# Turning half of x and the cross keys by square transposes and DMAs instead of TensorE

## The chip, the cores and the metric

The kernel runs on one NeuronCore of a Trainium2 chip (trn2). The metric is the device time of one execution, in microseconds, as the median of three runs. The kernel before takes 882.25 us (881.65 to 883.29).

## What is computed

Two transformer layers over 256 tokens of width 1024, in float32. The first mixes a gated delta rule with an indexed sparse attention and ends in a squared-relu feed-forward; the second mixes retention with a forgetting attention, then attends to 256 memory rows, then ends in a gated feed-forward. Cut to the places that the change touches:

```
x  = x + square(relu(rms_norm(x) @ w_mlp_up)) @ w_mlp_down      # first feed-forward
h  = rms_norm(x, g_mix_2);  p = h @ w_in_2                      # x is wanted with features on partitions
q, k, v, gate (retention), q, k, v, f (forgetting) = split(p)
mem: kv = rms_norm(mem, g_mem_2) @ w_xkv_2;  k = rms_norm per head of 256, * g_xk
x  = x + mixed @ w_out_2
q  = rms_norm(rms_norm(x, g_xattn_2) @ w_xq_2 per head of 256) * g_xq
x  = x + (softmax(q @ k.T / 16) @ v) @ w_xo_2                   # 4 heads, 256 memories
x  = x + (silu(h @ w_gate_2) * (h @ w_up_2)) @ w_down_2
```

In the first layer the delta rule needs the inverses of 16 triangular 128x128 matrices (two halves of the tokens, eight heads). The kernel builds them from solved 16x16 bases by products of blocks that double in size.

## The kernel before

It is written by hand: each engine has its own instruction list, and named semaphores order them. The order on an engine is the order of its code; nothing is planned at run time.

**Matrix products.** Every large product runs as three products of two-part numbers: `w_hi` and `w_lo` are the high and low part of the weights, `s_hi` and `s_lo` those of the activations, and hi*hi, hi*lo and lo*hi are summed in PSUM. A product is cut into blocks of up to 512 output columns (`B_DN`, `B_DN + 1`, `B_2`, ...), a block into chunks of 512 rows of the weight matrix, and the chunks go round four slots. SyncE loads a chunk into its slot when the products of the chunk four places earlier are finished (L450); ScalarE writes `w_hi` (L1303); VectorE writes `w_lo` (L1872); TensorE works on a chunk in two quarters of 12 products each (L540). `begin(b)` in ScalarE's and VectorE's lists stands for the splits of the chunks that block b still lacks and of the first two of block b+1; `project` copies a finished block out of PSUM, `residual` adds it to x.

**Turning.** A product wants the activations with features on partitions, and x lies with tokens on partitions. So after each residual TensorE turns x by 16 transposes of 128x128 against the identity into four PSUM banks, four to a bank (`turn`, L603). ScalarE scales them by the norm's gain into `s_hi` (`turn_hi`, L1342) and VectorE writes the rest into `s_lo` (`turn_lo`, L1909). The cross keys and queries are turned by TensorE too (`cross_operands`, L1191), and ScalarE and VectorE copy them out.

**Squares and DMAs.** The memory rows, the retention operands and the hidden rows of the last feed-forward go another way: VectorE transposes each 32x32 square in place (`turn_squares`, L1927) and GpSimd issues 16 DMAs that carry the squares to their bands of 32 partitions (`move`, L373).

**The order around the change.** While block `B_DN + 1` runs (eight chunks), ScalarE and VectorE split its weights. Then x is finished, TensorE turns it and runs `B_2`. ScalarE's list behind the turn: the load of the retention weights (1.5 MB, `act.dma_start(WR, ret_w)`), the squares for two norms, the splits of `B_2 + 1`. GpSimd moves the memory blocks in four bands, one behind each of four splits. VectorE rotates the retention queries and keys (L1937 to L1942) behind `project(B_2 + 1)` and then splits `B_2 + 3`. In the cross attention TensorE runs `B_XQ`, waits for the scaled keys (`x_k`), turns them (16 transposes), runs quarter 0 of `B_XQ + 1`, turns two query operands, runs quarter 1, and then starts `cross_logits(0)` (L1213). In the inverse, TensorE makes the products of step 0 (L921), waits for copies of ScalarE (L1594) and VectorE (L2283), makes those of step 1 (L922), turns the queries p = 2 and 3 (`queries_back`, L796), and runs quarter 2 of `B_GA`.

## Time and profile before

| | |
|---|---|
| median of 3 runs | 882.25 us (881.65 to 883.29) |
| the profiled execution | 883.71 us, its span 881.9 us |
| instructions | 12721 |
| TensorE busy | 873.5 us, 5023 matmuls and transposes |
| VectorE busy | 601.1 us |
| ScalarE busy | 439.4 us |
| GpSimd busy | 183.2 us |
| granted TensorE clock, mean | 0.998 |

The span is the time between the first and the last instruction of the profiled execution; the execution's own time is 1.8 us longer. Busy times are sums of an engine's instructions. Matmuls overlap each other, so their mean length is more than the step from one to the next; for the cost of one, the step is what counts. A row of a timeline merges instructions of one kind and gives start, length and, in square brackets, the idle time before it with what ended it.

### The profile page before, as it was taken

The page shows a single profiled execution, that of the slowest core. Times are in us where ns is not written, and L with a number is a line of the kernel's source. Part 1 is how long each engine was busy: PE and PEld are TensorE (multiplying, and loading weights), DVE is VectorE, ACT ScalarE, POOL GpSimd, SP SyncE. Part 2 cuts the span into 40 slices and gives each one's busy share as a digit, 9 for nine tenths or more (in the row PEclk, how much of TensorE's full clock was granted, in tenths as well). Part 3 has the DMA queues.
Part 4 walks back from the last instruction along what each step waited for, and adds up shares of the span by engine and source line. Part 5 has one row for each costly group of instructions (what it writes and reads, how often), then busy time and mean ns, then how long its engine had stood idle before and what let it go on. Part 6 is the DMA issues. An engine that isn't in the chain of part 4 may idle for free.

```text
span 881.9 us, 12721 instructions
## 1 busy us (share of the span) xinstructions
PE 873.5 (99%) x5023; PEld 751.7 (85%) x5023; DVE 601.1 (68%) x875; ACT 439.4 (50%) x613; POOL 183.2 (21%) x214
## 2 busy tenths in 40 slices
PE   9999999999999999999999999999999999999998
PEld 6897888888988999988888789888888888888886
DVE  5478988998696666745454948977785566665742
ACT  6365456864545555533344426546554544443531
POOL 0432234863110000000004222100100024444500
PEclk9999999999999999999999999999999999999999
DMA  8874542445146655655569765523542567775862
GB/s 297 200 258 144 191 144 87 132 129 166 48 139 195 193 191 190 190 191 191 190 212 258 201 165 192 189 98 118 170 142 79 164 199 218 219 220 160 254 218 72
DMA packets 87651, 154.67 MB, mean 175 GB/s; under 512 B 10528, under 2 KB 18512, under 8 KB 87472
## 3 DMA queue, kind: packets, MB, share of 16 engines
q1 hardware_dynamic: 80352, 144.55, 51.1%
q0 software_dynamic: 4720, 5.86, 3.7%
q10 hardware_dynamic: 2528, 3.56, 1.2%
q8 instruction: 35, 0.57, 0.3%
q14 instruction: 16, 0.13, 0.0%
HBM read 147.53 MB, written 1.44 MB: 169 GB/s over the span
## 4 chain that ended last, share of the span: by engine, by line
PE 92%; DVE 5%; DMA 1%; ACT 1%; issue 1%; SPq 0%; DVEq 0%; ACTq 0%
PE gemm L540 68%; PE gemm L1048 5%; PE mixbank L1048 5%; DVE w_lo L1872 2%; PE mixbank L603 1%; PE mixbank L702 1%; DMA raw<-in_w_in_dram 1%; PE mixbank L727 1%; PE mixbank L808 1%; PE mixbank L1213 1%; DVE mix L2010 1%; PE gemm L1241 1%; PE mixbank L713 1%; PE mixbank L750 1%; PE mixbank L902 0%
## 5 line engine op out<-in xcount | busy, mean ns | idle before, releaser
L1872 DVE TENSOR_TENSOR w_lo<-raw,w_hi 128x2048 fp32r<-128x2048 f32 (+3 forms) x132 | 288.0, 2189 | 180.3 <-ACT w_hi L1303 180.1
L1303 ACT ACTIVATE w_hi<-raw 128x2048 fp32r<-128x2048 f32 (+3 forms) x140 | 255.4, 1833 | 204.7 <-DMA raw<-in_w_in_dram 57.1
L540 PE MATMUL gemm<-w_hi,s_hi 128*128 128x512 f32 (+3 forms) x784 | 208.6, 386 | 0.6 <-ACT s_hi L1339 0.3
L540 PE MATMUL gemm<-w_lo,s_hi 128*128 128x512 f32 (+3 forms) x784 | 201.9, 378 | 1.2 <-DVE w_lo L1872 1.2
L540 PE MATMUL gemm<-w_hi,s_lo 128*128 128x512 f32 (+3 forms) x784 | 202.1, 378 | 0.0
L540 PEld LDWEIGHTS gemm<-w_lo,s_hi 128*128 128x128 f32 x784 | 142.6, 188 | 29.2 <-DVE w_lo L1872 2.1
L540 PEld LDWEIGHTS gemm<-w_hi,s_lo 128*128 128x128 f32 x784 | 143.2, 189 | 27.7
L540 PEld LDWEIGHTS gemm<-w_hi,s_hi 128*128 128x128 f32 x784 | 140.5, 189 | 26.0 <-issue 1.7
L2743 POOL TENSOR_TENSOR sm<-sm 128x2 f32<-128x2 f32 (+5 forms) x13 | 21.6, 1663 | 400.9 <-DVE sm L1933 296.5
L373 POOL DMA_DIRECT2D hid_moved<-hid_blocks x96 | 54.7, 578 | 72.4 <-DVE hid_blocks L2685 70.1
L2737 POOL TENSOR_TENSOR w_lo<-raw,w_hi 128x2048 fp32r<-128x2048 f32 x8 | 36.8, 4614 | 36.1 <-ACT w_hi L1303 36.1
L1320 ACT ACTIVATE mix<-gemm,sm 128x512 f32<-128x512 f32 (+2 forms) x25 | 16.2, 649 | 41.7 <-PE gemm L540 41.7
L1048 PE MATMUL mixbank<-u_lo,w_hi 128*128 128x256 f32 x128 | 35.9, 280 | 0.0
L1048 PE MATMUL mixbank<-s_hi,w_lo 128*128 128x256 f32 x128 | 35.7, 279 | 0.0
L1048 PE MATMUL mixbank<-s_hi,w_hi 128*128 128x256 f32 x128 | 35.6, 278 | 0.0
L540 PE MATMUL gemm<-w_hi,hT_hi 128*128 128x512 f32 x128 | 34.7, 389 | 0.0
L540 PE MATMUL gemm<-w_hi,hT_lo 128*128 128x512 f32 x128 | 34.7, 389 | 0.0
L540 PE MATMUL gemm<-w_lo,hT_hi 128*128 128x512 f32 x128 | 34.7, 389 | 0.0
L1048 PE MATMUL gemm<-u_lo,w_hi 128*128 128x256 f32 x128 | 33.6, 280 | 0.0
L1048 PE MATMUL gemm<-s_hi,w_hi 128*128 128x256 f32 x128 | 33.5, 279 | 0.0
L1048 PE MATMUL gemm<-s_hi,w_lo 128*128 128x256 f32 x128 | 33.5, 279 | 0.0
L2137 DVE SCALAR_TENSOR_TENSOR mix<-mixbank,cw,mix 128x255 f32<-128x255 f32 (+2 forms) x72 | 29.0, 474 | 1.2 <-ACT mix L1465 1.2
(365 smaller groups left out, 1183.8 us busy)
## 6 DMA issues: line engine op xcount, KB each, us to landing
raw<-in_w_in_dram SPq DMA_DIRECT2D x40, 1024.0 KB, 5.2
raw<-in_w_mlp_up_dram SPq DMA_DIRECT2D x16, 1024.0 KB, 5.6
raw<-in_w_mlp_down_dram SPq DMA_DIRECT2D x16, 1024.0 KB, 5.1
raw<-in_w_gate_dram SPq DMA_DIRECT2D x10, 1024.0 KB, 5.3
raw<-in_w_up_dram SPq DMA_DIRECT2D x10, 1024.0 KB, 5.1
raw<-in_w_down_dram SPq DMA_DIRECT2D x10, 1024.0 KB, 5.4
raw<-in_w_out_dram SPq DMA_DIRECT2D x8, 1024.0 KB, 5.2
raw<-in_w_xkv_dram SPq DMA_DIRECT2D x8, 1024.0 KB, 5.1
```

The costliest lines, as they stand in the source:

```text
L373: eng.dma_start(d[32 * j:32 * j + 32, :, i, :], s[32 * i:32 * i + 32, :, j, :]).then_inc(sem(name), 16)
L540: return nc.tensor.matmul(G[b % 2][t][:, 0:width], lhs, rhs, start=kt == 0 and not (low_x or low_w), stop=kt == blk["kt"] - 1 and (low_x i ...
L603: last = nc.tensor.transpose(M[q][:, (2 * kk + t) * P:(2 * kk + t + 1) * P], src(2 * q + kk, t), ident)
L702: last = nc.tensor.matmul(M[g % 2][:, j * ns:(j + 1) * ns], qq[:, P * t:P * t + P], kk[:, 0:ns], start=e == 0, stop=e == len(parts) - 1)
L713: last = nc.tensor.transpose(M[2][:, c * P:(c + 1) * P], exps[:, g % 2, c * P:(c + 1) * P], ident)
L1048: return nc.tensor.matmul(UP_BANKS[b % 2][f][:, 0:SEQ], w, (u_lo if low_x else s_hi)[:, kt, :], start=kt == 0 and not (low_x or low_w), st ...
L1303: nc.scalar.activation(w_hi[:, n % SLOTS, 0:kn, 0:width], raw[:, n % SLOTS, 0:kn, 0:width], ACT.Copy)\
L1320: nc.scalar.activation(dst, G[b % 2][0][:, 0:blocks[b]["n"]], ACT.Copy, scale=scale).then_inc(sem("ev0"), 1)
L1872: V.tensor_tensor(w_lo[:, s, 0:kn, 0:width], raw[:, s, 0:kn, 0:width], w_hi[:, s, 0:kn, 0:width].bitcast(F32), ALU.subtract)\
L2137: ins = V.scalar_tensor_tensor(y, M[CONV_BANK[s]][:, SEQ * j:SEQ * j + SEQ - tap], cw[:, 3 - tap, ct:ct + 1], y, ALU.mult, ALU.add)
L2737: pool.tensor_tensor(w_lo[:, s, 0:kn, 0:width], raw[:, s, 0:kn, 0:width], w_hi[:, s, 0:kn, 0:width].bitcast(F32), ALU.subtract)\
L2743: pool.tensor_tensor(dst, src, MHALF[:, 0:n], ALU.pow).then_inc(sem("root"), 1)
```

## The change

1. **Half of x.** While `B_DN + 1` runs, VectorE transposes the squares of the finished first half of x (two instructions, into the free hidden buffer), GpSimd moves them by 16 DMAs ahead of `norm_power(2)`, and ScalarE and VectorE make parts 0 to 3 of `s_hi` and `s_lo` from them (`moved_hi`, `moved_lo`). TensorE runs quarter 0 of `B_2` ahead of the turn, and turns only banks 2 and 3.
2. **Cross keys.** VectorE scales the keys between the two splits of `B_XQ` (eight instructions of 256 columns instead of four of 1024), and transposes their squares behind `mean_squares(4)`; GpSimd moves them by 16 DMAs behind `norm_power(4)`. The 16 transposes on TensorE and the four copies behind them go. `cross_logits` waits for all 16 DMAs.
3. **Reordered releases.** The load of the retention weights stands behind `project(B_2 + 1)`. The memory blocks are moved in eight parts of two DMAs. On VectorE `after_r`, `gates_hi` and `gates_lo` are made behind `begin(B_Q + 4)` instead of ahead of `project(B_Q + 2)`. In the inverse, `turn_square(1)` stands behind VectorE's copies for step 1, and `queries_back(2)` and `(3)` stand between the products of step 0 and step 1.

The diff, cut to its core:

```diff
+        X_BLOCKS = view(ar2, 12304, NT * D)
+        X_MOVED = view(ar2, T0 + 2048, NT * D)
-        def move(eng, dst, src, name, bands=range(4)):
+        def move(eng, dst, src, name, bands=range(4), targets=range(4)):
...
-                for j in range(4):
+                for j in targets:
                     eng.dma_start(d[32 * j:32 * j + 32, :, i, :], s[32 * i:32 * i + 32, :, j, :]).then_inc(sem(name), 16)
+        def x2_part(n):
+            return hid[:, n].rearrange("p f n -> p (f n)")
...
@@ tensor: inverse
                     if step == 1:
+                        if half == 0:
+                            for p in range(2, 4):
+                                queries_back(p)
                         pe.wait_ge(sem("inv_pc"), 2 + half + 1)
...
-            for p in range(2, 4):
-                queries_back(p)
             mm(B_GA, quarters=[2])
@@ tensor: behind the first feed-forward
-            turn(xtile, lambda q: [("ev0", B_DN + 1 + q // 2), ("ev1", B_DN + 1 + q // 2), ("hid_lo", 16)])
-            for j in range(4):
-                mm(B_2 + j, turned=None if j else 16)
+            mm(B_2, turned=16, quarters=[0])
+            turn(xtile, lambda q: [("ev0", B_DN + 2), ("ev1", B_DN + 2), ("hid_lo", 16)], banks=range(2, 4))
+            mm(B_2, turned=16, quarters=[1, 2, 3])
+            for j in range(1, 4):
+                mm(B_2 + j)
@@ tensor: cross attention
-            pe.wait_ge(sem("x_k"), 1)
-            cross_operands(range(4))
...
             def cross_logits(k):
...
+                pe.wait_ge(sem("x_moved"), 16 * 16)
...
+                        last = nc.tensor.matmul(o, xqT[:, 2 * h + e, P * t:P * t + P], moved(X_MOVED, 2 * h + e), start=e == 0, stop=e == 1)
@@ scalar
+            def moved_hi(v, name, norm, pairs):
+                for q in pairs:
+                    act.wait_ge(sem(name), 16 * 16)
+                    for kt in (2 * q, 2 * q + 1):
+                        ins = nc.scalar.activation(token_tile(s_hi[:, kt, :]), moved(v, kt), ACT.Copy, scale=gains[:, NORMS[norm], kt:kt + 1])
+                    sig(ins, "turn_hi")
...
             begin(B_DN + 1)
-            turn_hi(NORMS["mix2"])
+            moved_hi(x2_part(1), "x2_moved", "mix2", range(2))
+            turn_hi(NORMS["mix2"], banks=range(2, 4))
             act.wait_ge(sem("ev0"), B_2)
             act.wait_ge(sem("ev1"), B_2)
-            act.dma_start(WR, ret_w).then_inc(sem("ret_w_in"), 16)
...
                 project(B_2 + k, P2R[:, 0, NCOL * k:NCOL * k + NCOL], rs2)
+                if k == 1:
+                    act.dma_start(WR, ret_w).then_inc(sem("ret_w_in"), 16)
...
-            cross_operand(0)
-            cross_operand(2)
             query_sums(0)
@@ vector
-            V.tensor_copy(after_r[:, :], cst[:, C_AFTER:C_AFTER + P])
...
-            link(V.tensor_copy(gates_hi[:, :], GA_))
-            V.tensor_tensor(gates_lo[:, :], GA_, gates_hi[:, :].bitcast(F32), ALU.subtract).then_inc(sem("gdn_g"), 1)
             project(B_Q + 2, PQ[:, 1, NCOL * 2:NCOL * 3], RS[:, 1:2])
...
             begin(B_Q + 4)
+            V.tensor_copy(after_r[:, :], cst[:, C_AFTER:C_AFTER + P])
+            dve.wait_ge(sem("gdn_g"), 1)
+            link(V.tensor_copy(gates_hi[:, :], GA_))
+            V.tensor_tensor(gates_lo[:, :], GA_, gates_hi[:, :].bitcast(F32), ALU.subtract).then_inc(sem("gdn_g"), 1)
             select(range(4))
...
-            turn_square(1)
             for half in range(2):
                 dve.wait_ge(sem("inv_p"), 2 + 2 * half + 2)
                 V.tensor_copy(PS[96:128, 8 * half:8 * half + 8, 64:96], corner_bank(half, 1)[96:128]).then_inc(sem("inv_pd"), 1)
+            turn_square(1)
...
                 begin(B_DN + j)
+                if j == 1:
+                    moved_lo(x2_part(1), "mix2", range(2))
...
+                if j == 0:
+                    for t in range(NT):
+                        dve.wait_ge(sem(f"ev{t}"), B_DN + 1)
+                        ins = V.transpose(x2_part(0)[:, NCOL * t:NCOL * t + NCOL], x[:, t, 0:NCOL])
+                    ins.then_inc(sem("squares_turned"), 1)
-            turn_lo(NORMS["mix2"])
+            turn_lo(NORMS["mix2"], banks=range(2, 4))
...
             residual(B_O2, 0)
-            begin(B_O2 + 1)
+            link(V.tensor_tensor(vec[:, V_XK:V_XK + 256], vec[:, V_XK:V_XK + 256], vec[:, V_XQ:V_XQ + 256], ALU.mult))
+            split(B_XQ, 0)
+            dve.wait_ge(sem("root"), root("xk"))
+            for t in range(NT):
+                for h in range(4):
+                    k = KV[:, t, 256 * h:256 * h + 256]
+                    ins = V.scalar_tensor_tensor(k, k, RNX[:, 4 * t + h:4 * t + h + 1], vec[:, V_XK:V_XK + 256], ALU.mult, ALU.mult)
+            link(ins)
+            split(B_XQ, 1)
             residual(B_O2 + 1, 1)
             turn_lo(NORMS["xattn"])
             mean_squares(4)
...
+            turn_squares(X_BLOCKS, KV).then_inc(sem("squares_turned"), 1)
@@ gpsimd
             norm_power(1)
+            pool.wait_ge(sem("squares_turned"), 2)
+            move(pool, x2_part(1), x2_part(0), "x2_moved")
             norm_power(2)
...
-            for i, (b, c) in enumerate(((B_2, 1), (B_2 + 1, 1), (B_2 + 2, 0), (B_2 + 2, 1))):
-                pool.wait_ge(sem("split_hi"), blocks[b]["chunk0"] + c + 1)
-                move(pool, MEM, mem_blocks[:, :], "mem_moved", [i])
+            for n in range(8):
+                pool.wait_ge(sem("split_hi"), blocks[B_2 + 1]["chunk0"] + n)
+                move(pool, MEM, mem_blocks[:, :], "mem_moved", [n // 2], range(2 * (n % 2), 2 * (n % 2) + 2))
...
             norm_power(4)
+            pool.wait_ge(sem("squares_turned"), 4)
+            move(pool, X_MOVED, X_BLOCKS, "x_moved")
```

## Rows read from the trace of the kernel before

**Rows 1.** The page's part 1 (busy times), and part 4 (the chain that ended last).
```profile
PE 873.5 (99%) x5023; PEld 751.7 (85%) x5023; DVE 601.1 (68%) x875; ACT 439.4 (50%) x613; POOL 183.2 (21%) x214
...
PE 92%; DVE 5%; DMA 1%; ACT 1%; issue 1%; SPq 0%; DVEq 0%; ACTq 0%
```

**Rows 2.** TensorE's waits: who ended them; us in total, times, longest.
```profile
PE gemm L540 <- DVE w_lo L1872: 1.2, 2, 1.0
PE mixbank L922 <- DVE mix L2283: 0.6, 1, 0.6
```

**Rows 3.** The chain in order of time: start us, length us, what.
```profile
456.89 0.87 PE mixbank L603 x8
457.78 1.06 PE mixbank L603 x8
458.84 10.93 PE gemm L540 x48
...
643.48 1.75 PE mixbank L1191 x16
...
651.58 1.73 PE mixbank L1213 x8
```

**Rows 4.** Timeline of VectorE (first row) and TensorE around 100 us.
```profile
98.59 0.23 DVE L2026 CAST after_r<-cst 128x128 fp32r<-128x128 f32 x1
...
107.74 1.20 PE L540 MATMUL gemm<-w_lo,s_hi 128*128 128x512 f32 x4 [0.21 <-DVE w_lo L1872]
```

**Rows 5.** The chain in order of time, 212 to 224 us.
```profile
212.31 2.94 PE gemm L540 x12
...
218.40 1.46 PE gemm L796 x8
219.86 3.94 PE gemm L540 x12
```

**Rows 6.** TensorE by stretches: us, busy (instructions), granted clock, DMA share, GB/s.
```profile
220.00:221.00 1.00, 1.00 (x4) 0.50 0.01 2
...
881.00:882.00 1.00, 0.00 (x0) 0.51 0.00 0
...
493.00:494.00 1.00, 0.33 (x2) 1.00 0.65 154
```

**Rows 7.** Timelines of VectorE (first, last row) and ScalarE around the second mixer's start.
```profile
453.33 2.29 DVE L1872 TENSOR_TENSOR w_lo<-raw,w_hi 128x2048 fp32r<-128x2048 f32 x1 [3.18 <-ACT w_hi L1303]
...
459.16 1.23 ACT L1342 ACTIVATE s_hi<-mixbank,gains 128x256 fp32r<-128x256 f32 x3
...
464.94 3.71 ACT L1303 ACTIVATE w_hi<-raw 128x2048 fp32r<-128x2048 f32 x2
...
543.31 1.67 DVE L1918 SCALAR_TENSOR_TENSOR s_lo<-mix,gains,s_hi 128x256 fp32r<-128x256 f32 x4
```

**Rows 8.** VectorE's timeline, and DMA issues of 462 to 490 us (median landing).
```profile
481.86 2.29 DVE L1872 TENSOR_TENSOR w_lo<-raw,w_hi 128x2048 fp32r<-128x2048 f32 x1 [3.19 <-ACT w_hi L1303]
...
raw<-in_w_in_dram SPq DMA_DIRECT2D x5, 1024.0 KB, 10.0
```

**Rows 9.** Timelines of VectorE and GpSimd: what prices the key blocks.
```profile
626.75 2.29 DVE L1872 TENSOR_TENSOR w_lo<-raw,w_hi 128x2048 fp32r<-128x2048 f32 x1 [2.34 <-ACT w_hi L1303]
...
630.70 0.69 DVE L1897 TENSOR_TENSOR x<-gemm,x 128x512 f32<-128x512 f32 x1 [0.67 <-PE gemm L540]
...
636.49 0.42 DVE L2564 TENSOR_TENSOR vec<-vec 128x256 f32<-128x256 f32 x1
...
411.87 2.49 DVE L1927 STREAM_TRANSPOSE mem_blocks<-mem_rows 128x512 f32<-128x512 f32 x4
...
502.04 7.70 POOL L373 DMA_DIRECT2D mix<-mix  x12 [17.34 <-DVE mix L1927]
```

**Rows 10.** Landing times of the moves (L373): 513 to 520, then 460 to 520 us.
```profile
DMA to landing us min/median/max: 2.3/3.1/4.1
DMA to landing us min/median/max: 2.3/5.5/8.4
```

More of the change, by code:

```diff
@@ L1189, in cross_operands @@
                             c = P * (2 * (e % 4) + j)
-                            src = (KV if e < 4 else XQ)[:, t, c:c + P]
-                            last = nc.tensor.transpose(M[CROSS_BANK[e]][:, (2 * j + t) * P:(2 * j + t + 1) * P], src, ident)
+                            last = nc.tensor.transpose(M[CROSS_BANK[e]][:, (2 * j + t) * P:(2 * j + t + 1) * P], XQ[:, t, c:c + P], ident)
                     last.then_inc(sem("xT_pe"), 1)
             mm(B_XQ, turned=28)
-            pe.wait_ge(sem("x_k"), 1)
-            cross_operands(range(4))
             def cross_logits(k):
                 t, heads = WORK_X[k]
-                pe.wait_ge(sem("xT_act"), 3 if k < 2 else 4)
-                pe.wait_ge(sem("xT_dve"), 3 if k < 2 else 4)
+                pe.wait_ge(sem("x_moved"), 16 * 16)
+                pe.wait_ge(sem("xT_act"), 1 if k < 2 else 2)
+                pe.wait_ge(sem("xT_dve"), 1 if k < 2 else 2)
                 if k >= 2:
@@ L1212, in cross_logits @@
                     for e in range(2):
-                        last = nc.tensor.matmul(M[k % 2][:, SEQ * j:SEQ * j + SEQ], xqT[:, 2 * h + e, P * t:P * t + P], xkT[:, 2 * h + e, :],
-                                                start=e == 0, stop=e == 1)
+                        o = M[k % 2][:, SEQ * j:SEQ * j + SEQ].rearrange("p (t n) -> p t n", n=P)
+                        last = nc.tensor.matmul(o, xqT[:, 2 * h + e, P * t:P * t + P], moved(X_MOVED, 2 * h + e), start=e == 0, stop=e == 1)
                 last.then_inc(sem("att_logits"), 1)
@@ L1320, in project @@
                 nc.scalar.activation(dst, G[b % 2][0][:, 0:blocks[b]["n"]], ACT.Copy, scale=scale).then_inc(sem("ev0"), 1)
-            def memory_hi(pairs):
-                for q in pairs:
-                    act.wait_ge(sem("mem_moved"), 16 * 16)
-                    for kt in (2 * q, 2 * q + 1):
-                        ins = nc.scalar.activation(token_tile(s_hi[:, kt, :]), moved(MEM, kt), ACT.Copy, scale=gains[:, NORMS["mem"], kt:kt + 1])
-                    sig(ins, "turn_hi")
+            def moved_hi(v, name, norm, pairs):
[4 more added lines that the diff above has]
+                    sig(ins, "turn_hi")
+            def memory_hi(pairs):
+                moved_hi(MEM, "mem_moved", "mem", pairs)
             def turned_by_pe():
-                return seen.get("turn_hi", 0) + 1 - (KT // 2 if seen.get("turn_hi", 0) >= 20 else 0)
+                n = seen.get("turn_hi", 0)
+                return n + 1 - (2 if n >= 14 else 0) - (KT // 2 if n >= 20 else 0)
             def turn_hi(norm=None, banks=range(4)):
@@ L1911, in turn_lo, with moved_lo @@
                     sig(ins, "turn_lo")
-            def memory_lo(pairs):
+            def moved_lo(v, norm, pairs):
                 for q in pairs:
@@ L1917, in memory_lo @@
                     for kt in (2 * q, 2 * q + 1):
-                        ins = V.scalar_tensor_tensor(token_tile(s_lo[:, kt, :]), moved(MEM, kt), gains[:, NORMS["mem"], kt:kt + 1],
+                        ins = V.scalar_tensor_tensor(token_tile(s_lo[:, kt, :]), moved(v, kt), gains[:, NORMS[norm], kt:kt + 1],
                                                      token_tile(s_hi[:, kt, :]).bitcast(F32), ALU.mult, ALU.subtract)
                     sig(ins, "turn_lo")
+            def memory_lo(pairs):
+                moved_lo(MEM, "mem", pairs)
             def turn_squares(dst, src):
@@ L2562, in _ @@
             mean_squares(4)
-            link(V.tensor_tensor(vec[:, V_XK:V_XK + 256], vec[:, V_XK:V_XK + 256], vec[:, V_XQ:V_XQ + 256], ALU.mult))
-            dve.wait_ge(sem("root"), root("xk"))
-            kv = [KV[:, t, 0:D].rearrange("p (h d) -> p h d", d=256) for t in range(NT)]
-            for t in range(NT):
-                ins = V.tensor_tensor(kv[t], kv[t], spread(RNX[:, 4 * t:4 * t + 4], 2, 256), ALU.mult)
-            link(ins)
-            for t in range(NT):
-                ins = V.tensor_tensor(kv[t], kv[t], spread(vec[:, V_XK:V_XK + 256], 1, 4), ALU.mult)
-            ins.then_inc(sem("x_k"), 1)
+            turn_squares(X_BLOCKS, KV).then_inc(sem("squares_turned"), 1)
             dve.wait_ge(sem("root"), root("xattn"))
```

29 lines of the change are left out of this document (11 added, 18 removed).

## The prediction, written before the change was built

> **What bounds the kernel.** I read the page's parts 1 and 4 first: TensorE is busy 873.5 of 881.9 us, and 92% of the chain that ended last is TensorE's [rows 1]. Next, TensorE's waits: VectorE's low weights hold it for 1.2 us in two places (0.2 near 107 us, 1.0 near 494 us), and a copy for step 1 of the inverse for 0.6 us [rows 2]. So two things pay: work taken off TensorE, and the few waits and slow stretches it has. Third, the chain in order of time, for what one step costs. Eight transposes take 0.87 us, sixteen keys' transposes 1.75 us, so 0.11 us each and not the 0.27 us of their mean length; the second half of x's turn takes 1.06 us instead of 0.87 because it waits for the last residual [rows 3]. Fourth, the granted clock by stretches: it is full almost everywhere, but falls to 0.50 (1.2 GHz) near 219 us, where 12 products take 3.94 us and eight transposes 1.46 us, against 2.94 us for twelve just before [rows 5, 6].
>
> **Part A, gates later.** VectorE reaches the low weights wanted at 107.74 us late by 0.21 us [rows 4]. Taking `after_r` (0.23 us) and the two small copies from ahead of them covers that. Between zero (another step of VectorE's list ends last) and 0.4 us; I take 0.2. The three come back behind the next splits; the one who waits for the gates is GpSimd, idle there.
>
> **Part B, the inverse.** TensorE waited 0.6 us for VectorE's copy for step 1 [rows 2], which stood behind `turn_square(1)`. Now eight transposes stand in the gap and the copy comes first, so the 0.6 us go. What `turn_square(1)` feeds is wanted only after the next quarter of `B_GA`. The slow stretch followed at once: the eight transposes took 1.46 instead of 0.87 us and the twelve products 3.94 instead of about 2.9 [rows 3, 5], 1.6 us together. Before the clock fell TensorE had done 32- and 64-wide products and waited. Denser work should keep the clock. I take 0.6 + 1.6 = 2.2 us; the low end is 0.6, when the clock falls all the same.
>
> **Part C, half of x.** Eight transposes (0.87 us) and the wait of the second half (1.06 - 0.87 = 0.19) leave the path, since quarter 0 of `B_2` (10.93 / 4 = 2.73 us) now stands ahead of the turn [rows 3]: 1.06 us. What hides the added work: GpSimd's 16 DMAs start behind `B_DN`, some 35 us ahead of their use, so their issue and landing cost nothing. `moved_hi` and `moved_lo` (four instructions each, 1.67 us for four on VectorE) stand behind the last splits, at 455.6 us on VectorE [rows 7]. With the two residuals of 0.75 us behind them that ends at about 458.7 us; TensorE wants the residuals at 456.8 + 2.73 = 459.5 us. That cover is 0.8 us; were it gone, every further tenth would be a tenth of wait.
>
> ScalarE, though, turns banks 2 and 3 later: four instructions from about 460.1 to 461.6 us, where it had finished at 460.4 [rows 7]. The norm squares and then the splits of `B_2 + 1` (464.94 us in rows 7) move back by 1.2 to 1.4 us: high part ready at 468.2, low part 2.29 us later at 470.5 us. TensorE reaches `B_2 + 1` at 456.8 + 0.87 + 10.93 = 468.6 us and wants the low part 1.8 us on, at 470.4. I take 0.2 us of new wait, between zero and 0.6.
>
> **Part C, the stall at 494 us.** It begins with slow loads: 10.0 us to landing at 462 to 490 us, because the retention load and the memory moves share the engines; so the low part of `B_2 + 2` starts at 481.86 [rows 8], `project`, the rotation and the next low part follow it, and TensorE waits 1.0 us [rows 2]. With the retention load behind `project(B_2 + 1)` and the moves in pairs, I expect landing in 5 to 6 us and the low part some 3 us earlier, before `project(B_2 + 1)` is due: the 1.0 us go. The late load now meets the chunks of `B_2 + 3` and `B_2 + 4`; even 10 us to landing leaves them over 2 us. Between zero gained and 1.0; I take 1.0. Part C in all: 1.06 - 0.2 + 1.0 = 1.86 us.
>
> **Part D, cross keys.** Gain: 1.75 us of transposes [rows 3]; the copies and VectorE's 4.7 us of scaling were hidden. Costs: (1) VectorE scales keys in front of the last residual of `B_O2 + 1`, for which the turn waits. Nine instructions of 0.34 to 0.42 us, 3.1 to 3.8 us, must fit into idle time of 2.34 and 0.67 us and a further 0.3 between them [rows 9]; 0 to 0.5 us too late, I take 0.2.
>
> (2) `cross_logits(0)` waits for all 16 DMAs. In the times of before: VectorE is free at 636.49 [rows 9], four transposes of squares take 2.49 us, GpSimd starts about 0.2 us later, 639.2 us. Twelve DMAs take it 7.70 us [rows 9], 0.64 each, so the sixteenth is issued at 639.2 + 15 * 0.64 = 648.8 us. DMAs of the same size landed 2.3 to 4.1 us after issue with little beside them, 5.5 us in the median with the weight loads [rows 10]; here two 1 MB loads run beside, with pauses. I take 3.9 us: 652.7 us. TensorE reaches the logits at 651.58 - 1.75 = 649.8 us [rows 3]. So it waits 2.9 us, between 1.3 (landing 2.3) and 7.4 (8.4). Behind the waiting matmul stand all of the cross attention and the output product; nothing later in TensorE's list can pass. Nothing gives this wait back. Part D: 1.75 - 0.2 - 2.9 = -1.35 us.
>
> The Trainium skill (DMA: Bandwidth & Descriptors, Anatomy of one DMA and Why small descriptors are slow) puts a DMA at about 2.0 us plus its bytes at 436 GB/s, and says that copies within SBUF don't suffer from small pieces. For 64 KB that would be 2.15 us, an estimate from that page; the keys would land at 651.0 us and part D would come to +0.4 us. The quiet minimum of 2.3 us agrees with the page, the median of 5.5 us doesn't.
>
> **Sum.** 0.2 + 2.2 + 1.86 - 1.35 = 2.9 us off. Against the profiled execution (span 881.9 us, itself 883.71 us) that gives 880.8 us. That execution was 1.46 us above the median of 882.25 us; the same 2.9 us off the median give 879.3 us.
>
> **Rivals.**
>
> 1. The clock falls in the cross attention. At the end of the span, some 3 us after TensorE's last product, the clock was at 0.51; with 1.0 us of waiting near 494 us it stayed at 1.00 [rows 6]. The new wait of 2.9 us lies between. A fall like that of 219 us costs another 1.6 us: 880.9 us. For it, the wait's length; against it, the dense products on both sides. The Trainium skill (TensorE: Matmul & The Clock Gate, What's actually happening) says that half rate is the default and only activity lifts it. By that rule too an idle spell brings the fall.
>
> 2. The clock falls in the inverse all the same: the small products remain. Part B is then 0.6 instead of 2.2: 880.9 us. With rival 1 as well, 882.5 us.
>
> 3. Slower: the key blocks land last by far. The moves take engines that the two loads want too, and the 16th DMA lands after 8.4 us, the longest in rows 10. The wait is 7.4 us instead of 2.9, and the clock falls for 1.6 us: 879.3 + 4.5 + 1.6 = 885.4 us. The change loses as soon as the wait passes 2.9 + 2.9 = 5.8 us, or 4.2 us when the clock falls too. For it: each move carries 128-byte pieces, and loads beside such moves took 10.0 us [rows 8]. Against it: there the 1.5 MB load ran as well.
>
> 4. The key blocks land fast, 2.3 us after issue; the wait is 1.3 us: 877.7 us.
>
> 5. The shift of the retention load moves the collision instead of ending it, and TensorE waits 1.0 us for low weights in `B_2 + 3` or `B_2 + 4` as it did: 880.3 us.
>
> **Chances.** My forecast, 879.3 us (with 878.0 to 880.6 as its own range): 0.38. Rival 1: 0.20. Rival 2: 0.09, both 0.07. Rival 3: 0.12. Rival 4: 0.09. Rival 5: 0.05. The range 877.0 to 883.0 us leaves out rival 3 and a little of rival 4. A measurement of this kernel can tell 0.2%, 1.8 us, from no change. Faster by more (under 880.5 us): nine tenths of the forecast's chance, all of rival 4, two fifths of rivals 1, 2 and 5, together 0.55. Slower by more: nearly all of rival 3 and a little of the pair, 0.13. The rest, 0.32, is within.
>
> **What would show it.** TensorE's row for the transposes of x counts 72 instead of 80, and that for the cross operands 16 instead of 32. Part A: no idle time before the product at about 107 us. Part B: granted clock 1.00 from 216 to 223 us. Part C: quarter 0 of `B_2` directly behind `B_DN + 1`, loads there landing in 5 to 6 us, no wait of 1.0 us. Part D: a wait of 1.3 to 4.5 us before the first L1213 product, ended by the key DMAs, with the first move some 10 us ahead of the last. The prediction is wrong if that wait isn't there or passes 5 us, if the clock falls in it, or if a new wait for low weights shows in `B_2 + 1` to `B_2 + 4` beyond 0.6 us.

## The result: 888.84 us, slower by 0.7%

| | before | after |
|---|---|---|
| median | 882.25 us (881.65 to 884.02, 7 runs) | 888.84 us (885.19 to 889.88, 7 runs) |
| profiled execution, its span | 883.71, 881.9 us | 889.52, 887.3 us |
| instructions | 12721 | 12711 |
| TensorE busy, instructions | 873.5 us, 5023 | 871.7 us, 4999 |
| mean granted clock | 0.998 | 0.994 |

The ratio is 1.0068 [1.0055, 1.0081]. The forecast was 879.3 us, faster; the time lies above its range and 3.4 us above its slower rival. All comparisons here and below leave out the few executions that ran at a far lower granted clock.

The page after, parts 1 and 4, against [rows 1]:

```profile
span 887.3 us, 12711 instructions
...
PE 871.7 (98%) x4999; PEld 749.7 (84%) x4999; DVE 600.6 (68%) x883; ACT 438.6 (49%) x611; POOL 203.0 (23%) x246
...
PE 94%; ACT 2%; POOL 1%; DMA 1%; DVE 1%; issue 0%; ACTq 0%; DVEq 0%
```

TensorE does 24 instructions less and is busy 1.8 us less, yet the span is 5.4 us longer: the loss is waiting, not work. GpSimd and the keys' DMA are now in the chain. TensorE's rows for the transposes of x and for the cross operands count 72 and 16, as forecast. TensorE's waits after (columns as in [rows 2]) name it:

```profile
PE mixbank L1216 <- DMA mix<-mix: 8.3, 1, 8.3
...
PE mixbank L927 <- ACT mix L1607: 0.6, 1, 0.6
```

Neither of the waits for low weights of [rows 2] is among them, and the wait for VectorE's copy in the inverse is now one for ScalarE's. To see where each part's share lies, I read the start of the same work off both chains, from TensorE's rows that begin at it. Lines move by a few: L545 is L540 of before, L608 is L603, L1195 is L1191, L1216 is L1213. The chain after:

```profile
116.68 1.78 PE mixbank L707 x16
...
206.69 1.99 PE mixbank L907 x64
...
227.18 2.76 PE gemm L545 x12
...
521.45 1.93 PE mixbank L1118 x16
...
607.58 19.06 PE gemm L545 x84
...
635.96 8.98 POOL mix L374 x14
644.95 9.24 DMA mix<-mix
654.23 3.78 PE mixbank L1216 x8
658.01 3.43 PE gemm L545 x12
661.45 1.73 PE mixbank L1216 x8
...
703.68 180.25 PE gemm L545 x840
```

| the same work starts at | before | after | gained so far |
|---|---|---|---|
| first attention, L707 | 117.10 | 116.68 | 0.4 |
| inverse, L907 | 207.21 | 206.69 | 0.5 |
| behind the inverse, L545 x12 | 229.19 | 227.18 | 2.0 |
| forgetting attention, L1118 | 525.45 | 521.45 | 4.0 |
| last products of the second mixer, L545 x84 | 611.60 | 607.58 | 4.0 |
| `cross_logits(0)`, L1216 | 651.58 | 654.23 | -2.7 |
| `cross_logits(1)`, L1216 | 656.06 | 661.45 | -5.4 |
| last feed-forward, L545 x840 | 698.27 | 703.68 | -5.4 |

Parts A, B and C gained 4.0 us against this one execution of before (how much of that is the change, the experiments show). Part D lost 9.4 us, all between the last products of the second mixer and `cross_logits(1)`: 8.3 us of wait, and then 8 logits in 3.78 us instead of 1.73 [rows 3] and 12 products in 3.43 instead of the usual 2.75, together 2.7 us more, less the 1.75 us of transposes. The last 0.2 us is the turn of x in front, 2.23 us on TensorE's timeline and 2.06 before. TensorE by stretches (columns as in [rows 6]) says why those were slow:

```profile
640.00:642.00 2.00, 2.00 (x11) 1.00 0.91 125
648.00:650.00 2.00, 0.00 (x0) 0.78 0.94 176
650.00:652.00 2.00, 0.00 (x0) 0.50 1.04 274
...
654.00:656.00 2.00, 1.77 (x4) 0.50 0.08 32
656.00:658.00 2.00, 2.00 (x6) 0.50 0.00 0
658.00:660.00 2.00, 2.00 (x8) 0.66 0.00 0
```

The granted clock fell to 0.50 (1.2 GHz) while TensorE did nothing, and is still 0.50 at 656 to 658 us with TensorE busy again: the price of the fall is paid behind the wait. Last, the transfers. GpSimd's row of the timeline, the moves' landing times, and the DMA view of 634 to 656 us (queue: packets, MB, share of sixteen engines; below it the issues with their median landing):

```profile
635.26 10.34 POOL L374 DMA_DIRECT2D mix<-mix  x16 [1.93 <-DVE mix L1936]
...
DMA to landing us min/median/max: 4.1/6.2/9.2
```

```profile
q1 hardware_dynamic: 1584, 3.15, 45.2%
q0 software_dynamic: 512, 1.05, 36.6%
...
raw<-in_w_xo_dram SPq DMA_DIRECT2D x3, 1024.0 KB, 10.0
mix<-mix POOLq DMA_DIRECT2D x16, 64.0 KB, 6.2
```

The last move was issued at 644.95 us and landed 9.2 us later. In these 22 us the moves held the sixteen engines for 36.6%, 8.1 us in all, and the three weight loads for 45.2%, 9.9 us. Together that is 18.0 us for all sixteen engines, nearly all of it between 635.3 and 654.2 us, which is 18.9 us. These are the times that packets took, and packets of two queues overlap (the share at 644 to 646 us was 1.23), so they measure how crowded the engines were and not pure work. SyncE issued the three loads at 634.2, 639.7 and 646.0 us: the second among the moves, the third 1.1 us behind the last of them.

### The profile page after: what moved, and what is told of

Read it like the earlier page. It is cut to its first block, busy times and chain, and to the rows that moved or that the text cites. A ratio compares the mean times of both kernels' runs of the same rounds, so it can differ in the third digit from the quotient of the medians.

```text
span 887.3 us, 12711 instructions
## 1 busy us (share of the span) xinstructions
PE 871.7 (98%) x4999; PEld 749.7 (84%) x4999; DVE 600.6 (68%) x883; ACT 438.6 (49%) x611; POOL 203.0 (23%) x246
## 4 chain that ended last, share of the span: by engine, by line
PE 94%; ACT 2%; POOL 1%; DMA 1%; DVE 1%; issue 0%; ACTq 0%; DVEq 0%
PE gemm L545 71%; PE gemm L1054 5%; PE mixbank L1054 5%; PE mixbank L707 1%; PE mixbank L608 1%; POOL mix L374 1%; DMA mix<-mix 1%; PE mixbank L1216 1%; PE mixbank L732 1%; PE mixbank L813 1%; PE gemm L1243 1%; ACT w_hi L1305 1%; PE mixbank L718 1%; ACT s_hi L1348 1%; ACT junk L1358 1%; PE mixbank L755 1%
## 5 line engine op out<-in xcount | busy, mean ns | idle before, releaser
L545 PE MATMUL gemm<-w_hi,s_hi 128*128 128x512 f32 (+3 forms) x784 | 208.5, 386 | 0.6 <-ACT s_hi L1345 0.3
L545 PE MATMUL gemm<-w_lo,s_hi 128*128 128x512 f32 (+3 forms) x784 | 201.7, 377 | 0.1
L545 PE MATMUL gemm<-w_hi,s_lo 128*128 128x512 f32 (+3 forms) x784 | 201.7, 377 | 0.0
L545 PEld LDWEIGHTS gemm<-w_hi,s_lo 128*128 128x128 f32 x784 | 142.8, 188 | 27.6
L545 PEld LDWEIGHTS gemm<-w_lo,s_hi 128*128 128x128 f32 x784 | 142.6, 188 | 27.8 <-DVE w_lo L1878 0.5
L545 PEld LDWEIGHTS gemm<-w_hi,s_hi 128*128 128x128 f32 x784 | 140.5, 189 | 26.3 <-issue 1.8
L374 POOL DMA_DIRECT2D hid<-hid x16 | 9.3, 591 | 132.4 <-DVE hid L2447 132.4
L545 PE MATMUL gemm<-w_hi,hT_hi 128*128 128x512 f32 x128 | 34.7, 389 | 0.0
L545 PE MATMUL gemm<-w_hi,hT_lo 128*128 128x512 f32 x128 | 34.7, 389 | 0.0
L545 PE MATMUL gemm<-w_lo,hT_hi 128*128 128x512 f32 x128 | 34.7, 389 | 0.0
```

The costliest lines, as they stand in the source:

```text
L374: eng.dma_start(d[32 * j:32 * j + 32, :, i, :], s[32 * i:32 * i + 32, :, j, :]).then_inc(sem(name), 16)
L545: return nc.tensor.matmul(G[b % 2][t][:, 0:width], lhs, rhs, start=kt == 0 and not (low_x or low_w), stop=kt == blk["kt"] - 1 and (low_x i ...
```

## The experiments

Line numbers differ by a few from kernel to kernel. Each block names its time, its range over so many executions, and the ratio to the kernel before on the same chip. The kernel before had 882.25 us beside e1 to e4, 882.1 beside e5, e6, e8 and e9, and 881.77 beside e7, e10, e11 and e12; kernels of one such group compare directly, across groups I give 1 us to either side.

**Part D undone, and part D alone.** `e1_keys_on_pe` is the changed kernel without part D:

```diff
-                pe.wait_ge(sem("x_moved"), 16 * 16)
+            pe.wait_ge(sem("x_k"), 1)
+            cross_operands(range(4))
```

> The changed kernel with part D alone undone: TensorE turns the cross keys as before; half of x, the gates, the inverse and the retention load stay as changed. My theory: in the two traces the changed kernel was 4.0 us ahead when it reached the cross attention and everything lost was lost there. So this kernel keeps the 4.0 us and takes 882.25 - 4.0 = 878.2 us (877.6 to 878.9), with the granted clock at 1.00 through the cross attention. Rival: some of the loss comes with the other edits (GpSimd's moves of x, the later retention load); then 880 us or more.

Measured: 879.62 us (879.11 to 880.61, 12), 0.9971 [0.9959, 0.9983]. That is above my range and just below the rival's 880: the loss does come with part D alone, but parts A to C gain 2.6 us in the median and not 4.0. The span of its profile is 877.3 us, 4.6 below that of before. The difference between 4.6 and 2.6 lies in the execution of before that was profiled. Of 62 executions of the kernel before beside the experiments, 37 had a mean granted clock of 1.000 and a median of 881.3 us, and 18 had 0.998 and 883.0 us. The profiled one had 0.998 and 883.71 us, with the slow stretch near 219 us of [rows 5, 6]. The mean clock says that most executions don't have it; against those, A to C gain 1.7 us.

`e2_keys_only` is the kernel before with part D alone.

> The kernel before with part D alone: the cross keys by squares and 16 DMAs. My theory: the traces give part D +1.75 us of transposes off, -8.3 us of waiting for the DMAs and -2.7 us of slow clock behind the wait, -9.4 us in all with the turn; alone it does the same: 882.25 + 9.4 = 891.6 us (889.5 to 892.5), a wait of 7 to 9 us before the first product of keys and queries. Rival: the loss needs the other edits (the loads stand differently by then); then the wait is near the 2.9 us that I forecast and the time 883.6 us.

Measured: 888.99 us (888.03 to 891.7, 6), 1.0089 [1.0073, 1.0105]. Its row for the keys:

```profile
653.77 3.78 PE L1209 MATMUL mixbank<-mix 128*128 128x256 f32 x8 [5.59 <-DMA mix<-mix]
```

Part D costs 6.7 us by itself, with the same 3.78 us of slow logits behind the wait. The wait is 5.6 us, and both it and the time are below my ranges: moves and loads are issued at the same distances as in the changed kernel, yet the last move lands after 6.6 us here and 9.2 there. So A to C gain and D loses, and neither needs the other; the size of D's loss differs with the landing.

This kernel has the inverse of before, in the old order and with the same wait of 0.59 us for VectorE's copy, so its trace is a second look at it. TensorE by stretches, and the chain where the inverse starts and behind it:

```profile
218.00:220.00 2.00, 2.00 (x27) 1.00 0.83 316
```

```profile
207.07 1.99 PE mixbank L903 x64
...
227.61 2.76 PE gemm L541 x12
```

The clock stays at 1.00 here. From the start of the inverse to the row behind it, it is 20.54 us; the profile of before has 21.98, the changed kernel with the new order 20.49. So in these traces the new order by itself gains 0.05 us, and the other 1.4 us are the slow stretch of one execution.

**Is it the loads that the moves share the engines with?** `e3_small_loads` cuts only the bytes of the `B_XO` loads to an eighth (64 of 512 columns, loads and splits alike, so the last product is not the reference's):

```diff
+                if b in (B_XO, B_XO + 1):
+                    width = 64
```

> The changed kernel, but the four loads of the cross output weights bring 64 of each 512 columns (and their splits are as narrow), so an eighth of the bytes moves beside the key blocks; the rest of the weights is stale data, so the last results aren't the reference's. Theory 1, contention: the moves landed 9.2 us after issue because these 1 MB loads were on the same DMA engines. Then the last move lands 2.5 to 4.1 us after issue, the wait before the first product is 1.5 to 3 us, the clock stays at 1.00, and the time is 880 to 881.5 us. Theory 2, the moves themselves (16 at once, in pieces of 128 bytes): the landing stays at 6 us or more, the wait at 5 us or more, and the time at 885 us or above.

Measured: 880.0 us (879.43 to 880.17, 10), 0.9979 [0.997, 0.9988]. The moves' landing and the row for the keys:

```profile
DMA to landing us min/median/max: 2.2/2.5/3.3
...
647.20 1.99 PE L1218 MATMUL mixbank<-mix 128*128 128x256 f32 x8 [1.20 <-DMA mix<-mix]
```

With the bytes gone the moves land in 3.3 us at most, the last in 2.2, 1.2 us of wait are left, the logits run at full clock, and 8 to 9 us of the time are back (8.8 by the medians, 7.9 by the ratios). The sharing with the loads' bytes is the cause. The wait that remains comes from GpSimd's issue, 10.3 us for 16 moves in any case, and the 2.2 us of the last landing.

**Moves first, loads behind.** `e4_moves_first` lets SyncE issue the 16 moves ahead of the `B_XO` loads:

```diff
+                if (b, c) == (B_XO, 0):
+                    sp.wait_ge(sem("squares_turned"), 4)
+                    move(sp, X_MOVED, X_BLOCKS, "x_moved")
-            move(pool, X_MOVED, X_BLOCKS, "x_moved")
```

> The changed kernel, but SyncE issues the 16 key moves, directly ahead of the first load of the cross output weights, instead of GpSimd. SyncE's issue step is 0.37 us against GpSimd's 0.65, so the last is issued 5.6 us after the first and not 9.7, and no load stands among them. Theory 1, contention and issue order: the keys are in place 9.5 to 10.5 us after the squares, the wait at the first product is 0 to 1 us and the clock stays up; but the second load of the output weights comes late and the exponentials stand behind its split on ScalarE, which costs 1 to 2 us in place of it: 878 to 880.5 us. Theory 2, the moves are slow by themselves: the wait stays above 4 us, 884 us or more.

Measured: 888.39 us (887.59 to 888.73, 6), 1.0074 [1.0062, 1.0087]. A miss, and a useful one. SyncE's timeline, the landing of the moves, TensorE's two largest waits there, and ScalarE's timeline:

```profile
634.91 10.85 SPq L374 DMA_DIRECT2D mix<-mix  x16
...
DMA to landing us min/median/max: 2.1/2.3/2.4
```

```profile
PE mixbank L1229 <- DVE mix L2628: 5.8, 1, 5.8
...
PE mixbank L1219 <- DMA mix<-mix: 1.4, 1, 1.4
```

```profile
651.41 1.91 ACT L1308 ACTIVATE w_hi<-raw 128x2048 fp32r<-128x2048 f32 x1 [8.06 <-DMA raw<-in_w_xo_dram]
654.09 1.91 ACT L1308 ACTIVATE w_hi<-raw 128x2048 fp32r<-128x2048 f32 x1 [0.77 <-DMA raw<-in_w_xo_dram]
656.54 0.56 ACT L1773 ACTIVATE mix<-mixbank,sm 128x256 f32<-128x256 f32 x1 [0.54 <-DVE sm L2620]
```

The wait for the keys fell to 1.4 us, a little over the 0 to 1 that I expected. But the loads now start at 645.8 us, and their splits stand ahead of the softmax's exponentials in ScalarE's list: ScalarE waits 8.06 us for the load, the exponentials come at 656.5 us, and TensorE waits 5.8 us for what follows from them, and the clock falls again (0.50 at 658 to 662 us). What the moves win the splits lose. I had named this step and priced it at 1 to 2 us; it cost 5.8 us of wait and the fall behind it.

**One load beside the moves.** `e5_load_held` keeps the moves on GpSimd, holds the second `B_XO` load until the moves have landed, and puts its splits behind the last exponentials (ScalarE) and copies (VectorE):

```diff
+                if (b, c) == (B_XO, 1):
+                    sp.wait_ge(sem("x_moved"), 16 * 16)
...
-            split(B_XO, 1)
             cross_exp(3)
+            split(B_XO, 1)
```

> The changed kernel, with the second load of the cross output weights held until the key blocks have landed, and the two splits of that chunk behind the last exponentials and copies, where their engines idle. GpSimd still issues the moves, and only the first 1 MB load runs beside them. Theory 1 (contention): the last moves land 2.3 to 3.5 us after issue, the wait before the keys' product is 1.2 to 2.5 us, the clock stays at 1.00, no new wait behind it, and the time is 879.5 to 881.5 us. If the load that does the harm is the first one, the wait stays at 4 us or more and the clock falls: 884 us or more.

Measured: 879.81 us (879.44 to 880.47, 12), 0.9976 [0.9967, 0.9985], as expected. TensorE by stretches:

```profile
644.00:646.00 2.00, 2.00 (x10) 1.00 0.62 103
646.00:648.00 2.00, 0.82 (x5) 1.00 0.45 66
```

The wait is 1.2 us, the moves land in 2.2 to 5.0 us, and the clock stays at 1.00 through it. Part D's loss is gone, 8 to 9 us, with no byte and no move less than in the changed kernel. The edit holds more than one load: the third stands behind the second in SyncE's list, so they are issued at 647.6 and 648.0 us, where the changed kernel has 639.7 and 646.0. Which of the two does the harm no run here tells apart; the first alone does not. Part D now about breaks even with part D undone (879.62).

**Earlier squares.** `e6_held_early` is e5 with the keys' squares transposed behind the first of four banks of `turn_lo`, ahead of `mean_squares(4)`:

```diff
-            turn_lo(NORMS["xattn"])
-            mean_squares(4)
-            turn_squares(X_BLOCKS, KV).then_inc(sem("squares_turned"), 1)
+            turn_lo(NORMS["xattn"], banks=[0])
+            turn_squares(X_BLOCKS, KV).then_inc(sem("squares_turned"), 1)
+            turn_lo(NORMS["xattn"], banks=range(1, 4))
+            mean_squares(4)
```

> As the kernel with the load held, and VectorE transposes the squares of the keys behind the first quarter of its turn of x, 1.9 us earlier for GpSimd (which must still do the norm first). Theory: the moves are issued from 633.4 instead of 635.3 us and the wait goes to 0 to 0.6 us; the 1.75 us of transposes are then gained in earnest and the time is 877.8 to 879.3 us, below the kernel with the keys on TensorE (879.6). Rival: the later parts of the turn on VectorE are now late for TensorE or for the norm, a new wait of 1 to 2 us takes the place, and the time is 880 us or more.

Measured: 879.18 us (878.84 to 879.91, 9), 0.997 [0.996, 0.9981], within the range. The wait for the keys is 0.8 us, a little over what I expected, and one of 0.2 us for `s_hi` has grown to 0.5.

**What does the slow clock cost by itself?** Useless products ahead of `cross_logits(0)` fill the wait; the moves stay as they are. `e8_filler` has three, `e11_filler8` eight:

```diff
+                for _ in range(8):
+                    nc.tensor.matmul(G[B_XQ % 2][0][:, :], ident, x[:, 0, 0:NCOL], start=True, stop=True)
```

> The changed kernel with three products of no use (identity by x, 512 columns, about 1.9 us each) in TensorE's list directly ahead of the wait for the key blocks; they fill 5.7 of the 8.3 us. Theory: the wait shrinks to 2 to 3 us, the landing is the same, and the clock doesn't fall, so the 2.7 us of slow products behind the wait go: 888.8 - 2.7 = 886.1 us (885.3 to 886.9). Rival: the slow products behind the wait are slow for another reason (cold operands, the keys' own layout); then nothing changes: 888.3 us or more.

Measured: 888.08 us (886.11 to 888.96, 6), 1.0068 [1.0052, 1.0084]. Each product took 0.91 us, not the 1.9 us that I had reckoned with, so 3.8 us of wait were left and the clock fell to 0.50 in it; the logits took 3.78 us again. That doesn't tell the theories apart, so it was repeated with eight.

> The changed kernel with eight useless products ahead of the wait instead of three (0.91 us each as the trace of the last one showed, 7.3 us); with three, 3.8 us of waiting were left and the clock fell all the same. Theory: 0 to 1.5 us of waiting are left, the clock stays at 1.00, the eight products of keys and queries take 1.7 to 2.0 us instead of 3.8, and the time falls by 2.7 us to 886.1 us (885.0 to 887.0). Rival: the slow products have another cause; they take 3.8 us still, and the time is 888 us or more.

Measured: 885.6 us (885.27 to 886.49, 5), 1.0044 [1.0031, 1.0057]. TensorE's timeline:

```profile
645.44 7.03 PE L1251 MATMUL gemm<-x,cst 128*128 128x512 f32 x16
652.67 1.99 PE L1216 MATMUL mixbank<-mix 128*128 128x256 f32 x8 [0.20 <-DMA mix<-mix]
```

The clock stayed at 1.00 and the first logits take 1.99 us. From them to the second logits the chain has 4.7 us, and 7.2 in the changed kernel (654.23 to 661.45): the fall costs 2.5 us. The other 0.2 to 0.3 us of the 2.7 are in every kernel with part D at full clock: its first logits take 1.99 us (e3, e5, e6, e10, e11) where those of before take 1.73, and I did not follow up why. The start itself came 1.6 us earlier, since the moves landed in 8.1 us at most. The medians differ by 3.2 us, the ratios by 2.1.

**The inverse.** `e7_split_later` is e1 with ScalarE's split of `B_GA + 1`'s second chunk behind its four copies for step 1 of the inverse.

> The kernel with the keys on TensorE (879.6 us), and ScalarE's split of the last chunk of the second gate block behind its four copies for the last corners of the inverse, not ahead of them. Both kernels' traces show a wait of 0.6 us there that the kernel before didn't have (TensorE now comes 1.5 us earlier and meets ScalarE's split). Theory: the wait goes, 879.0 us (878.6 to 879.4), no other wait grows. Rival: another step (the squares of the queries on ScalarE, VectorE's copies) ends just behind it: no change.

Measured: 879.05 us (878.6 to 879.3, 5), 0.9966 [0.9953, 0.9978]. The 0.6 us of wait for ScalarE's copy are gone from TensorE's list. The time is 0.6 us below e12's in the same group, whose wait is still there, and below e1's; the intervals of the ratios overlap, so the size rests on the trace: from the start of the inverse to the row behind it 19.87 us, 20.53 in e1.

**Which edit of part C ended the stall at 494 us?** `e9_ret_early` is e1 with the retention load back in its early place; `e12_mem_fours` is e1 with the memory moves back in fours.

> The kernel with the keys on TensorE (879.6 us), but the load of the retention weights back where it was, ahead of the norm squares. Theory: that load is what made the weight loads of the second mixer take 10 us; with it back, loads there take 9 to 10 us again, TensorE waits about 1.0 us for low weights in the fourth block, and the time is 880.6 us (880.2 to 881.0). Rival: the moves of the memory blocks in pairs did it alone; then the time stays at 879.6 us and the loads land in 5 to 6 us.

Measured: 879.84 us (879.04 to 881.51, 12), 0.9979 [0.9969, 0.9988]. No wait for low weights came back, so my theory that only the load's new place ended it falls.

> The kernel with the keys on TensorE (879.6 us), but GpSimd moves the memory blocks as before in four bands of four DMAs, each band behind a split; the retention load stays late. With that load early and the moves in pairs the wait of 1.0 us at the fourth block of the second mixer did not come back. Theory now: the moves in pairs ended it, so here the weight loads take 8 us or more again and TensorE waits 0.5 to 1.0 us for low weights there: 880.1 to 880.6 us. Rival: either edit alone is enough; then no such wait, 879.6 us.

Measured: 879.62 us (879.36 to 880.28, 8), 0.9976 [0.9966, 0.9986]. No such wait either. What decides is when VectorE gets to the low weights behind its six rotations. Its rows for them before, in e1 and in e9:

```profile
491.99 4.49 DVE L1872 TENSOR_TENSOR w_lo<-raw,w_hi 128x2048 fp32r<-128x2048 f32 x2
```

```profile
485.25 2.29 DVE L1885 TENSOR_TENSOR w_lo<-raw,w_hi 128x2048 fp32r<-128x2048 f32 x1
```

```profile
488.00 4.49 DVE L1884 TENSOR_TENSOR w_lo<-raw,w_hi 128x2048 fp32r<-128x2048 f32 x2
```

A chunk takes 2.29 us, so it is ready at 487.5 us in e1, 488.0 in e12 and 490.3 in e9. TensorE gets to its product 31.1 us ahead of the forgetting attention, as the trace of before has it: at 489.7, 490.2 and 490.4 us. TensorE has 2.2, 2.2 and 0.1 us in reserve; before, the chunk was ready 1.1 us too late. So the place of the retention load is worth 2 us of reserve, the moves in pairs nothing here, and e9 escaped the wait narrowly. In e2, which has neither edit, the wait was 0.3 us and not 1.0, so part of that stall too belongs to the one execution. Whether it would come back with both edits undone and half of x in place was not run.

**The best of it.** `e10_best` is e6 with three of the 16 moves issued ahead of `norm_power(4)` on GpSimd, and e7's edit:

```diff
-            norm_power(4)
-            move(pool, X_MOVED, X_BLOCKS, "x_moved")
+            move(pool, X_MOVED, X_BLOCKS, "x_moved", [0], range(3))
+            norm_power(4)
+            move(pool, X_MOVED, X_BLOCKS, "x_moved", [0], [3])
+            move(pool, X_MOVED, X_BLOCKS, "x_moved", range(1, 4))
```

> The kernel with the load held and the squares early (879.2 us, wait 0.8 us), with two more edits: three of the 16 moves are issued ahead of the norm's power on GpSimd, while it waits for that norm anyway, and the split of the second gate block behind the copies of the inverse. Theory: the last move is issued some 2 us earlier, the wait at the keys' product is 0 to 0.2 us, and the wait of 0.6 us in the inverse goes: 879.2 - 0.8 - 0.6 = 877.8 us (877.3 to 878.4). Rival: moves earlier meet the load of the output weights and land later, and the norm is late: 879 us or more.

Measured: 877.64 us (877.32 to 878.55, 5), 0.9953 [0.994, 0.9966], as expected. The row for the keys has no idle time ahead of it:

```profile
644.77 1.99 PE L1218 MATMUL mixbank<-mix 128*128 128x256 f32 x8
```

It beats both kernels, the one before and the changed one. Against e7 of the same group, which has the same edit in the inverse but keys turned by TensorE, it gains 1.4 us by the medians and 1.1 by the ratios: with its waits gone part D is worth nearly the 1.75 - 0.2 us at which it was priced without them. The intervals of the ratios overlap, the executions themselves do not (878.55 us at most and 878.6 at least).

## Why the prediction was wrong

**The failed step is part D's cost (2), the landing of the last move.** Part D's other terms came out: cost (1), the late residual, was priced at 0.2 us and is the 0.17 by which the turn grew. I had the issue of the first move at 639.2 us in the times of before, which is 635.2 with 4.0 us gained ahead of it: 635.26. The sixteenth was due 9.6 us later: 644.95 less 635.26 is 9.7. TensorE was due at the logits at 649.8 - 4.0 = 645.8 us: it was there at 654.23 less its 8.27 us of idle time, 645.96. Then I took 3.9 us for the landing, and it took 9.2. The wait was 8.3 us instead of 2.9, and the clock fell in it, for 2.5 us more. Landing times of single moves [rows 10] were the wrong rows: they hold how busy the engines happened to be then. "Two 1 MB loads run beside" was wrong too: the third is issued when TensorE reaches the logits (651.61 us before, against 651.58), 1.1 us behind the last move, which was not yet in. What had to be added up is how long the engines are held. The trace of before had it, in the queue rows of its DMA view for 456 to 490 us:

```profile
q1 hardware_dynamic: 2991, 5.94, 64.3%
q0 software_dynamic: 511, 1.05, 19.8%
```

Sixteen moves of the same size hold all sixteen engines for 19.8% of 34 us, 6.7 us, 0.21 us for a packet of 2 KB. The loads hold them for 64.3% with 2991 packets, 0.12 us for one; three loads of 528 packets come to 11.6 us. An estimate from these rows is then 18.3 us from 635.3 on: 653.6 us, or 8.6 us behind the last issue. With two loads it is 14.4 us, 4.8 behind. Measured were 9.2 us in the changed kernel, and 6.6 (e2), 7.3 (e8) and 8.1 us (e11) with the same moves and loads. So the sum gives the size that rows 10 missed, and that it comes within 0.6 us of one execution is luck. The cause is shown by e3, which takes the loads' bytes away, and by e5, which holds back two loads.

By the fit in the Trainium skill (DMA: Bandwidth & Descriptors, Anatomy of one DMA) a move of 64 KB takes 2.15 us, an estimate from that page. By that rule the keys would have landed at 647.1 us; the trace agrees where the engines are quiet (2.1 to 2.4 us in e4, 2.2 in e3) and disagrees under load (4.1 to 9.2 in the changed kernel).

**Rival 3 was this mechanism**, at 0.12, with the longest landing of rows 10 (8.4 us; 9.2 measured) and a clock fall of 1.6 us (2.5 measured). Its time of 885.4 us was 3.4 short of the 888.84. What I held against it, that the 1.5 MB load ran beside the moves before, was wrong: three loads issued within 12 us were enough. Its break-even of 4.2 us with a fall was not tested closely: with parts A to C in place, waits of 1.2 us (e3, e5) gain and 8.3 us loses.

**Rival 1, the clock.** The fall came, but with a wait of 8.3 us and not with one of 2.9. Waits of 0.8 (e6), 1.2 (e3, e5) and 1.4 us (e4's for the keys) left the clock at 1.00; waits of 3.8 (e8), 5.6 (e2), 5.8 (e4's second) and 8.3 us brought it to 0.50. What a wait of 2.9 us would have done no run here shows.

**Part A.** Predicted 0.2, the two traces give 0.4 to 0.5. Its wait of 0.2 is gone. The rest is within the spread between executions: the first attention starts at 116.95 us in e2, which lacks part A, and between 115.89 (e1) and 116.73 (e9) in kernels that have it.

**Part B.** Predicted 2.2, the two traces give 1.5 (2.0 less 0.5), and this near hit is luck. The second look at the old order in e2 gives the edit 0.05 us; the rest is the slow stretch, which e2 doesn't have. So the 0.6 us did not go, though the wait for VectorE's copy did. The trace of TensorE and of ScalarE has what I missed:

```profile
222.87 0.27 PE L927 MATMUL mixbank<-mix 64*64 64x64 f32 x1 [0.62 <-ACT mix L1607]
...
220.46 1.96 ACT L1305 ACTIVATE w_hi<-raw 128x2048 fp32r<-128x2048 f32 x1
222.44 0.65 ACT L1607 ACTIVATE mix<-mixbank 64x256 f32<-64x256 f32 x2
```

The next copy on ScalarE stands behind a split of 1.96 us. As long as TensorE came later, by its wait for VectorE and in the profile of before by the slow stretch too, this step showed little or nothing: a wait of 0.2 us in e2, none before. I had looked only at the wait that I took away; e7 moves the split and gains the 0.6 us. And the 1.6 us for the slow stretch counted in full what the median holds only in part: I took the sum against one profiled execution and carried it over to the median unchanged, though its own distance of 1.46 us from the median was on the table. Of A to C's 4.3 us predicted and 4.0 in the table, 2.6 are left in e1 against the medians. That the clock stayed at 1.00 from 217 to 224 us after the change proves nothing by one trace, as e2's does the same in the old order. The executions say more: all 78 of the kernels with parts A to C and no long wait (e1, e3, e5 to e7, e9 to e12) had a mean clock of at least 0.999, of the 62 of the kernel before 21 had 0.998 or less. So rival 2 didn't come, and denser work is a likely reason; which of the edits keeps the clock no run separates.

**Part C.** Predicted 1.86, the trace gives 2.0 against the profile of before and 1.8 against e2's. Quarter 0 stands ahead of the turn, x's transposes are halved, and the small wait that I had forecast for the low part of `B_2 + 1` is there, 0.2 us: the chain runs through that split. TensorE's timeline at the turn, and the chain behind it:

```profile
457.42 1.03 PE L608 MATMUL mixbank<-cst,x 128*128 128x128 f32 x8
```

```profile
466.18 2.30 DVE w_lo L1878
468.53 52.92 PE gemm L545 x232
```

The loads of 458 to 490 us land in 6.5 us in the median instead of 10.0 [rows 8], a little above the 5 to 6 that I had expected, and the 1.0 us near 494 are gone; rival 5 didn't come. But the reason was half wrong: with one of the two edits undone the wait stayed away, the moves in pairs bought no reserve, and loads of 8.2 us in e12 did it as well.

No run undoes A, B or C alone; their shares rest on the starts in the traces of before, after and e2, and on e1 for the three together.

**A slip in the chances.** Nine tenths of 0.38, 0.09 and two fifths of 0.34 add up to 0.57, not 0.55.

## What to carry over

Before a transfer is put on the path, add up how long every transfer in its window holds the engines, not how long one took to land: moves of 64 KB in pieces of 128 bytes cost the engines about twice what their bytes do in a load. If the sum is longer than the cover, hold back loads whose data is wanted late, and move their splits behind the work that must not wait for them (e4 against e5). Such a sum is rough: here the same transfers landed 6.6 to 9.2 us behind the last issue. And when a wait is taken away, look at which step would have ended second. When a gain comes from a slow stretch, look first whether most executions have it: a second trace of the same code, or the mean clock of many executions, tells.

## What the runs showed of the hardware

- **Moves cost the engines about twice what their bytes do in a load.** A packet of 2 KB of a move took an engine 0.21 us before and 0.25 us after (8.1 us by 16 engines over 512 packets), and 0.22 us in e3, where the loads beside it had an eighth of their bytes; one of a weight load took 0.12 and 0.10 us.
- **SyncE needs 0.63 us to issue one such move** (the median in e4; sixteen took it 10.85 us). A load of 1 MB takes it 0.37 us after the change, and I had expected the same of the moves. GpSimd needs 0.65, so moving the issue over saved nothing.
- **From SyncE's queue the same moves are cut finer.** In 9 us of e4:

```profile
q1 hardware_dynamic: 6825, 0.85, 62.8%
...
mix<-mix SPq DMA_DIRECT2D x14, 64.0 KB, 2.3
```

  6825 packets of about 128 bytes for 0.85 MB, where GpSimd's queue has 512 packets for 1.05 MB. They held the engines for 62.8% of 9 us, 5.7 us.
- **A fall of the clock in a wait is paid behind it.** It cost 2.5 us here for one wait. Useless products in the wait (e11) kept the clock at 1.00 and won that back.
- **The same code can have a slow stretch in one execution and none in another.** The inverse in the old order had the clock at 0.50 near 220 us in the profile of before and at 1.00 in e2's.
- **The same transfers land differently.** With the same moves and loads at the same distances the last move landed 9.2 us after issue in the changed kernel and 6.6 in e2.
